# Forget-gate attention: the causal mask in the forget rows, a third bank for the scores, k's squares in halves, low weights by adding transfers

## The reference, cut to what matters

```python
q, k, v, z, f_logit = jnp.split(h @ w_in, ...)
q = rms_norm(q.reshape(b, s_len, 16, 128), q_norm_g)      # per head and token
k = rms_norm(k.reshape(b, s_len, 16, 128), k_norm_g)
c = jnp.cumsum(jax.nn.log_sigmoid(f_logit + f_bias), axis=1)
# per head, blocks of 128 queries:
logits = q_blk @ k.T * 128 ** -0.5 + c_blk[:, None] - c[None, :]
logits = jnp.where(k_pos <= q_pos, logits, -jnp.inf)
o = jax.nn.softmax(logits, axis=-1) @ v
out = (o * jax.nn.silu(z)) @ w_out
```

## Time and profile before

| | us |
|---|---|
| three runs, median (lowest, highest) | 2593.55 (2592.87, 2595.41) |
| profiled execution: span on the core | 2593.1 |
| TensorE busy (share of the span) | 2550.1 (98%) |
| VectorE, ScalarE, GpSimd busy | 1509.1, 1231.1, 1514.3 |

### The profile page before, as it was taken

One profiled execution on the slowest core, in us unless ns is written; L12 is line 12 of the kernel. 1 busy time (PEld: TensorE's weight loads), 2 busy tenths in 40 slices (PEclk: granted clock), 3 DMA queues, 4 the chain that ended last, 5 costly groups with the idle time before them and its releaser, 6 DMA issues.

```text
span 2593.1 us, 31711 instructions
## 1 busy us (share of the span) xinstructions
PE 2550.1 (98%) x12043; PEld 2055.1 (79%) x12043; DVE 1509.1 (58%) x2434; ACT 1231.1 (47%) x1944; POOL 1514.3 (58%) x935
## 2 busy tenths in 40 slices
PE   8999999999999999999999999999999999999998
PEld 6777787878778788888888887878876778788887
DVE  6999764165585714444450799976498744532202
ACT  5887645254564623222232588664335553422322
POOL 2999766444444366444455399966635547644653
PEclk9999999999999999999999999999999999999999
DMA  8776434434234133333333677543422242233221
GB/s 195 177 177 145 122 97 91 98 82 82 75 71 74 57 98 93 96 95 96 96 95 97 152 167 175 140 114 108 113 96 86 67 139 97 86 98 98 98 98 65
DMA packets 296440, 279.12 MB, mean 108 GB/s; under 512 B 17814, under 2 KB 258672, under 8 KB 296289
## 3 DMA queue, kind: packets, MB, share of 16 engines
q1 hardware_dynamic: 281472, 223.94, 31.0%
q0 software_dynamic: 14816, 53.16, 10.0%
HBM read 228.75 MB, written 5.84 MB: 90 GB/s over the span
## 4 chain that ended last, share of the span: by engine, by line
PE 82%; DVE 9%; ACT 4%; issue 2%; DMA 2%; POOL 1%; SPq 0%; DVEq 0%; POOLq 0%; ACTq 0%
PE ps L64 80%; DVE AR L81 4%; DVE AR L73 2%; PE ps L67 2%; DVE HL L81 1%; DMA WR<-in_a_w_in 1%; ACT L70 1%; ACT AR L70 1%; DMA WL<-WR 1%; ACT HT L70 1%; DVE X L73 1%; POOL AR L73 0%; DVE ps L81 0%; ACT WL L70 0%; ACT HH L70 0%
## 5 line engine op out<-in xcount | busy, mean ns | idle before, releaser
L73 POOL TENSOR_TENSOR WL<-WR,WH 128x1024 fp32r<-128x1024 f32 x324 | 818.8, 2547 | 762.6 <-ACT WH L70 762.6
L64 PE MATMUL ps<-HH,WH 128*128 128x512 f32 x3080 | 1226.7, 399 | 4.3 <-ACT HH L70 1.2
L64 PE MATMUL ps<-HL,WH 128*128 128x512 f32 x3080 | 1194.9, 391 | 1.3 <-DVE HL L81 1.3
L64 PE MATMUL ps<-HH,WL 128*128 128x512 f32 x3080 | 1096.1, 390 | 2.3 <-DMA WL<-WR 2.3
L64 PEld LDWEIGHTS ps<-HH,WH 128*128 128x128 f32 x3080 | 579.6, 188 | 146.6 <-issue 15.3
L64 PEld LDWEIGHTS ps<-HL,WH 128*128 128x128 f32 x3080 | 580.0, 188 | 127.0 <-issue 7.9
L64 PEld LDWEIGHTS ps<-HH,WL 128*128 128x128 f32 x3080 | 578.6, 188 | 123.8 <-DMA WL<-WR 2.7
L70 ACT ACTIVATE WH<-WR 128x1024 fp32r<-128x1024 f32 (+1 forms) x405 | 409.2, 1047 | 488.9 <-PE ps L64 443.0
L81 DVE SCALAR_TENSOR_TENSOR ps<-AR,CW,ps 128x512 f32<-128x512 f32 x654 | 454.6, 752 | 17.2 <-ACT ps L70 10.2
L73 POOL TENSOR_TENSOR AR<-AR 128x512 f32<-128x512 f32 x200 | 306.8, 1848 | 16.2 <-ACT AR L70 8.9
L70 ACT ACTIVATE AR<-ps 128x512 f32<-128x512 f32 (+3 forms) x265 | 131.9, 522 | 272.8 <-PE ps L64 176.5
(11 more groups left out here) (184 smaller groups left out, 2180.0 us busy)
## 6 DMA issues: line engine op xcount, KB each, us to landing
WR<-in_a_w_in SPq DMA_DIRECT2D x96, 512.0 KB, 5.2
WL<-WR POOLq DMA_DIRECT2D x81, 512.0 KB, 5.7
WR<-in_c_w_in SPq DMA_DIRECT2D x64, 512.0 KB, 5.4
WR<-in_a_w_out SPq DMA_DIRECT2D x16, 1024.0 KB, 4.9
WR<-in_b_w_in SPq DMA_DIRECT2D x16, 1024.0 KB, 8.4
WR<-in_b_w_in SPq DMA_DIRECT2D x32, 512.0 KB, 11.0
WR<-in_w_mlp_in SPq DMA_DIRECT2D x16, 1024.0 KB, 5.4
WR<-in_w_mlp_out SPq DMA_DIRECT2D x16, 1024.0 KB, 4.9
```

The costliest lines, as they stand in the source:

```text
L64: return Op(None if self.e is None else self.e.matmul(o, l, r, start=first, stop=last, skip_group_check=True))
L73: return Op(None if self.e is None else self.e.tensor_tensor(o, a, b, op))
```

## The change

The mask: `causal_gpsimd` sets -1e30 above the diagonal in CB itself, which is now one buffer of 1280 columns, a forget row of its own for each block (3, 2, 1, 0 in this order); the mask products, `caus` and `identr` go. `negc_rows` holds the rows in this layout, written by four stores. The select of `setup_gpsimd` for the mask goes, too. The scores: blocks 0, 1, 2, 3 use banks 4, 5, 2, 4 (head 15: 4, 5, 4, 5). k's squares: high and low halves as q's, by ScalarE, VectorE and GpSimd. Low weights: chunks of heads 1 to 15 are `summed`; GpSimd's and ScalarE's rounds take them half by half. QN and KN have one buffer, CB is fetched behind the last row maximum of the head before. MR, AR and DIAG are laid out anew.

```diff
         WL = sb("WL", 2 * 2048, F32R)
-        identr = sb("identr", P, F32R)
-        caus = sb("caus", P, F32R)
-        MR = sb("MR", 1280, F32R)
+        onesr = sb("onesr", P, F32R)
+        MR = sb("MR", 4 * T, F32R)
         ident = sb("ident", P)
...
-            return i == 0 and n == 1 or any(f < i < f + KE + (KE // 2 if n == 0 else 0) or i == f + KE + KE // 2 + 1 for f in FIRST_A)
+            return i == 0 and n == 1 or i in HEAD_CHUNK[1:] or any(f < i < f + KE + (KE // 2 if n == 0 else 0) or i == f + KE + KE // 2 + 1 for f in FIRST_A)
 
...
-            pool.memset(SM0, 0.0).then_inc(consts, "mask0")
-            pool.wait_ge(consts, "mask0")
+            pool.wait_ge(consts, "ident0")
             pool.select(ident[:, :], ALU.not_equal, 1.0, [[-1, P]], 1).then_inc(consts, "ident")
-            pool.select(SM0, ALU.is_ge, NEG, [[-1, P]], 1).then_inc(consts, "mask")
-            pool.wait_ge(consts, "mask")
-            pool.copy(identr[:, :], ident[:, :]).then_inc(consts, "identr")
-            pool.copy(caus[:, :], SM0).then_inc(consts, "caus")
             split_lo(pool, 0, (0,))
...
-        DIAG = [ar(A0 + 8 * T + i * P, P) for i in range(5)]
+        DIAG = [HT[:, i * P:(i + 1) * P] for i in range(5)]
...
-        b_cb = [sig("b_cb0"), sig("b_cb1")]
+        b_cb = sig("b_cb")
...
-        RAW, QN, KN, CB = ([ar(B1 + (2 * n + i) * T) for i in range(2)] for n in range(4))
-        NEGC = ar(B1 + 8 * T)
-        E8, BY2 = RB2, [RB, ar(B1 + 9 * T)]
-        LF, FB = ar(B1 + 10 * T, 64), ar(B1 + 10 * T + 64, 16)
-        BF, BAB, BEX, BMN = (ar(B1 + 10 * T + 80 + 64 * n, 64) for n in range(4))
-        TRI, FT = RAW[0], KN[0][0:16, :]
-        SQHI, SQLO, onesr = MR[:, 0:T], MR[:, T:2 * T], MR[:, 1024:1152]
-        negc_rows = nc.dram_tensor("negc_rows", (16, T), F32).ap()
-        V_CHUNK = [FIRST_B + 9 + 6 * g for g in range(4)]
-        HEAD_CHUNK = [FIRST_B + 9 + 6 * (h // 4) + 2 + h % 4 for h in range(16)]
+        RAW = [ar(B1 + i * T) for i in range(2)]
+        QN, KN = ar(B1 + 2 * T), ar(B1 + 3 * T)
+        CB, C_OFF = ar(B1 + 4 * T, 1280), [1152, 896, 512, 0]
+        NEGC = ar(B1 + 7 * T)
+        E8, BY2 = RB2, [RB, ar(B1 + 6 * T + 256)]
+        LF, FB = ar(B1 + 8 * T, 64), ar(B1 + 8 * T + 64, 16)
+        BF, BAB, BEX, BMN = (ar(B1 + 8 * T + 80 + 64 * n, 64) for n in range(4))
+        TRI, FT = RAW[0], KN[0:16, :]
+        SQHI, SQLO = ([MR[:, (2 * n + i) * T:(2 * n + i + 1) * T] for i in range(2)] for n in range(2))
+        negc_rows = nc.dram_tensor("negc_rows", (16, 1280), F32).ap()
 
         def values_tensor(pe, g):
             for part in range(2):
...
-                            pe.wait_ge(b_var, 4 * g - 2, 0)
+                            pe.wait_ge(b_ttr, 4 * g - 2, 2)
...
         def scores_tensor(pe, h):
-            s = h % 2
             pe.wait_ge(b_nrm, h, 0, 4)
             pe.wait_ge(b_nrm, h, 1, 4)
             for i in range(NB):
-                b, n = banks[4 + i % 2], (i + 1) * P
-                if i >= 2:
-                    pe.wait_ge(b_ttr, h, i - 2)
-                elif h:
-                    pe.wait_ge(b_ttr, h - 1, i + 2)
-                elif i:
-                    pe.wait_ge(b_e8)
+                if i == 0:
+                    pe.wait_ge(*((b_ttr, h - 1, 3) if h else (b_ft,)))
+                elif i == 1:
+                    pe.wait_ge(*((b_ttr, h - 1, 1) if h else (b_e8,)))
+                elif i == 2:
+                    pe.wait_ge(*((b_var, h, 0) if h < 15 else (b_ttr, h, 0)))
                 else:
-                    pe.wait_ge(b_ft)
-                pe.mm(b[:, 0:n], QN[s][:, i * P:(i + 1) * P], KN[s][:, 0:n], True, False)
-                pe.mm(b[:, i * P:n], identr[:, :], caus[:, :], False, True).then_inc(b_s, h, i)
+                    pe.wait_ge(b_ttr, h, 0 if h < 15 else 1)
+                pe.mm(logit_bank(h, i), QN[:, i * P:(i + 1) * P], KN[:, 0:(i + 1) * P], True, True).then_inc(b_s, h, i)
+
+        def logit_bank(h, i):
+            return banks[((4, 5, 2, 4) if h < 15 else (4, 5, 4, 5))[i]][:, 0:(i + 1) * P]
 
         def statistics_tensor(pe, h):
             if h == 0:
@@ -1501,10 +1497,12 @@
             else:
                 pe.wait_ge(b_var, h - 1, 0)
             pe.wait_ge(consts, "onesr")
+            if h:
+                pe.wait_ge(b_ttr, h - 1, 2)
             pe.wait_ge(b_sq, h, 0)
-            pe.wait_ge(b_sqlo, h, 1)
-            pe.mm(banks[2][:, :], onesr, SQHI, True, False)
-            pe.mm(banks[2][:, :], onesr, SQLO, False, True).then_inc(b_stat, h, 0)
+            pe.wait_ge(b_sqlo, h, 0, 1)
+            pe.mm(banks[2][:, :], onesr[:, :], SQHI[0], True, False)
+            pe.mm(banks[2][:, :], onesr[:, :], SQLO[0], False, True).then_inc(b_stat, h, 0)
             if h >= 2:
                 pe.wait_ge(b_ev, h - 2, 3)
             elif h == 1:
@@ -1512,7 +1510,9 @@
             else:
                 pe.wait_ge(rb_made, 1)
             pe.wait_ge(b_sq, h, 1)
-            pe.mm(banks[7][:, :], ones[:, :], SQS[1], True, True).then_inc(b_stat, h, 1)
+            pe.wait_ge(b_sqlo, h, 1, 1)
+            pe.mm(banks[7][:, :], onesr[:, :], SQHI[1], True, False)
+            pe.mm(banks[7][:, :], onesr[:, :], SQLO[1], False, True).then_inc(b_stat, h, 1)
...
         def normal_vector(dve, h):
-            s = h % 2
-            for half, (o, g) in enumerate(((QN[s], VQ[:, 0:1]), (KN[s], va["k_norm"]))):
+            for half, (o, g) in enumerate(((QN, VQ[:, 0:1]), (KN, va["k_norm"]))):
                 y, raw = BY2[half], RAW[half]
                 dve.wait_ge(b_y, h, 1, half)
-                if h >= 2:
-                    dve.wait_ge(b_s, h - 2, 3)
+                if h:
+                    dve.wait_ge(b_s, h - 1, 3)
                 dve.tt(o, y, y, ALU.mult).then_inc(b_nrm, h, half, 0)
                 dve.wait_ge(b_nrm, h, half, 0)
                 dve.stt(o, o, -0.5, VAR[half], ALU.mult, ALU.mult).then_inc(b_nrm, h, half, 1)
-                if half == 0:
-                    dve.wait_ge(b_sqlo, h, 0)
+                dve.wait_ge(b_sqlo, h, half, 0)
                 dve.stt(raw, raw, g, y, ALU.mult, ALU.mult).then_inc(b_nrm, h, half, 3)
                 dve.wait_ge(b_nrm, h, half, 3)
                 dve.stt(o, o, 1.5, raw, ALU.add, ALU.mult).then_inc(b_nrm, h, half, 4)
@@ -1620,13 +1618,13 @@
 
         def logits_vector(dve, h):
             small(4, "b_sum", h)
-            dve.wait_ge(b_cb[h % 2], h)
+            dve.wait_ge(b_mask, h, 1)
             for i in range(NB):
                 n = (i + 1) * P
                 dve.wait_ge(b_s, h, i)
                 if h:
                     dve.wait_ge(b_t, h - 1, i)
-                dve.ttr(BP[i], banks[4 + i % 2][:, 0:n], CB[h % 2][:, 0:n], -1.0, 3e38, ALU.add, ALU.min,
+                dve.ttr(BP[i], logit_bank(h, i), CB[:, C_OFF[i]:C_OFF[i] + n], -1.0, 3e38, ALU.add, ALU.min,
                         small(1, "b_max", h, i)).then_inc(b_ttr, h, i)
...
-                    split_hi(act, HEAD_CHUNK[h] + 1)
+                    split_hi(act, HEAD_CHUNK[h] + 1, (0,))
                     act.wait_ge(b_p, h, 0)
                     if h:
                         act.wait_ge(b_stat, h - 1, 0)
-                    act.act(SQHI, banks[0][:, :], ACT.Square).then_inc(b_sq, h, 0)
+                    act.act(SQHI[0], banks[0][:, :], ACT.Square).then_inc(b_sq, h, 0)
                 if h >= 2:
                     copy_turned_scalar(act, h - 2, 0)
                     copy_turned_scalar(act, h - 2, 1)
                 if h < 16:
+                    split_hi(act, HEAD_CHUNK[h] + 1, (1,))
                     act.wait_ge(b_p, h, 1)
                     if h:
                         act.wait_ge(b_stat, h - 1, 1)
-                    act.act(SQS[1], banks[1][:, :], ACT.Square).then_inc(b_sq, h, 1)
+                    act.act(SQHI[1], banks[1][:, :], ACT.Square).then_inc(b_sq, h, 1)
                 if h >= 2:
                     copy_turned_scalar(act, h - 2, 2)
                     copy_turned_scalar(act, h - 2, 3)
...
+        def forget_rows_gpsimd(pool, h):
+            pool.wait_ge(b_negc_out, NB - 1)
+            pool.dma(CB, bass.AP(negc_rows.tensor, h * 1280, [[0, P], [1, 1280]])).then_inc(b_cb, h, by=16)
+
+        def causal_gpsimd(pool, h):
+            pool.wait_ge(b_cb, h)
+            for n, (first, step) in enumerate(((384, 384), (1024, P))):
+                blocks = CB[:, first:first + 2 * step].rearrange("p (b c) -> p b c", c=step)[:, :, 0:P]
+                pool.select(blocks, ALU.is_ge, NEG, [[0, 2], [-1, P]], 1).then_inc(b_mask, h, n)
+
+        def square_low_gpsimd(pool, h, half):
+            pool.wait_ge(b_raw, h, half)
+            if h:
+                pool.wait_ge(b_stat, h - 1, half)
+                pool.wait_ge(b_sqlo, h - 1, half, 1)
+            pool.tt(SQS[half], RAW[half], RAW[half], ALU.mult).then_inc(b_sqlo, h, half, 0)
+            pool.wait_ge(b_sqlo, h, half, 0)
```

(41 more changed lines are left out.)

## The result

The change makes the kernel slower: 2614.54 us, median of 4 runs, against 2593.21 us before; the ratio is 1.008, 95% interval 1.0068 to 1.0092. The forecast was 2572.5 us. The profiled execution's span is 2616.3 us.

A forecast was written before the change was run, and what follows sets the result against it. TensorE, busy 2550.1 of 2593.1 us, was taken as the bound; ten plain intervals 18.5, three with values 4.1, start +0.5 and k's waits -1.8 sum to 21.3 us saved: 2572.5 us, range 2566 to 2584.

The forecast's parts named there:

- rival 4: Weight loads of the heads: no change, because shorter heads wait for loads that start later; 2593 us, chance 0.05.
- Rival 3: Low weights: adding transfers land late, at 11.0 us, so 13 heads wait 2.2 us each; 2601 us, chance 0.06.
- masks 0.52: Scores on TensorE: 64 mask products leave, 0.13 us a mask, saving 0.52 us a head.
- third bank 0.44: Block 2's scores, moved to bank 2, no longer wait for block 0's maximum: 0.44 us saved a head.
- k's sum 0.40: Sum of k's squares: two fp32r products replace one fp32 product of 512 columns, saving 0.40 us a head.
- hold-up 0.49: TensorE's wait for normalised k, made by GpSimd's subtractions holding up VectorE, goes: 0.49 us a head.
- The start: Head 0: 3.1 us of new waiting offset by a wait that goes; the next interval 18.7 us, +0.5 in all.
- k waits of 0.6 us: Second head after each values group: TensorE waits 0.6 us for k's low squares, three times, -1.8 us.
- Values intervals: Three head-to-head intervals with a values group have no wait before the scores: 1.36 us saved each, 4.1 in all.
- The tail: Last head: delayed early projection makes the last T 0.65 us later, the last scores give 0.65 back: 0.
- Rival 1: VectorE's chain: the hold-up only moves to GpSimd's selects and squares; heads 18.2 us apart, 2580 us, chance 0.12.
- Rival 2: GpSimd's queue bounds: every second head waits 2.6 us for k's low squares, some 10 us; 2582 us, chance 0.11.

The follow-up runs named there:

- the run with c_w_in's rows: Changed kernel with the heads' q and k weights fetched from c_w_in (rows 32,768 B apart, not 32,832 B; other values): 2582.4 us, ratio 0.995.
- the even pitch: Changed kernel with the q and k chunks fetched from the same b_w_in at a row pitch of 32,768 B instead of 32,832 B: 2582.8 us, 0.9955.
- the runs with repaired order: Changed kernel with whole chunks behind heads 3, 7, 11, 15 and `part_low` before the last forget rows: 2575.8 us with c_w_in's rows, 2608.7 with real rows.

## Why the prediction was wrong

- **The step that failed** is in the forecast's sentences on when the low weights are wanted and in rival 4: "Each next weight load starts some 5 us later than now; one takes 11.0 us and has about 19", "a load would have to take 19 us". 11.0 us is a median over halves, and over heads of which a half has faster loads. For heads 4 to 7 and 12 to 15 the k halves take 12.8 to 25.4 us in the trace of before, and in the changed kernel 13.4 to 26.0. I read the median and not the spread, which the same profile gives as 4.7/9.6/25.4.
- **The bound of the adding transfers**, 4.5 to 9.3 us, came from 81 transfers in other stages, beside loads with even pitch. Beside a slow load they took 12 to 24 us. Rival 3 had the mechanism (they land as the loads do), its price (11.0 us, from the same median) and a chance of 0.06. It named an argument against itself that did not bear: "none of the trace's 81 passed 9.3", when none of the 81 had such a load beside it: they belong to other mixers, whose loads of 512 KB have medians of 5.2 and 5.4 us. Rivals 3 and 4 also work together, which I hadn't joined: the next load waits until the adding transfer has left its slot, so one that is late makes the next load late.
- **Its size.** Interval by interval, in the profiled executions (spans 2616.3 and 2578.2 us; the medians are 32 us apart), the changed kernel loses 37.5 us to the run with c_w_in's rows. By the waits, TensorE stood 24.9 us for WL<-WR. The rest is laid to the clock: 0.95 in the stretch of 535 to 930 us against 0.98 in the run with c_w_in's rows and in that with the even pitch, 0.03 of 395 us, about 12 (a rough estimate, since idle time counts in it).
- **TensorE's terms** (masks 0.52, third bank 0.44, k's sum 0.40, hold-up 0.49) held together: 1.89 us measured against 1.85, in every undisturbed head. The four were not measured one by one. For the ten intervals: 19.0 against 18.5 us.
- **The start**: k's sum waited 3.5 us in head 0 (forecast 3.1). The next interval was 17.13 to 17.15, where I had 18.7: GpSimd was ready for it.
- **k waits of 0.6 us** in the second head behind a values group: none in the even-pitch run, the interval is 17.35. The forecast took 1.8 us off for nothing.
- **Values intervals**: 1.36 each forecast, 0.07 measured with c_w_in's rows (40.63 to 40.56). I had costed the half-by-half order at nothing; in the values rounds it puts the second half's subtraction behind q's squares. With the order repaired they gave 1.85, but took 1.6 from the head before.
- **The tail**: forecast 0, measured 7.4 us (22.0 against 14.6). I had seen `part_low` stand behind the last forget rows and priced it at 0.65 us for the next T, without asking what TensorE does meanwhile: nothing, and the clock falls.
- **Rival 1** (the hold-up only moves) holds for heads beside subtractions alone, at 2.79 us in the changed kernel's head 7 and at 18.99 in the runs with repaired order. **Rival 2** (GpSimd's queue) holds without the adding transfers: 30.1 us.

In sum, on loads that land in 4 to 9 us the time is 2582.4 us, and the forecast would have missed by 10 too. By intervals the tail was 7.4 us and the values rounds 3.9 short; the start, the k waits and the ten heads gave 3.9 back, so 13.9 us were gained of the 21.3. The other 32 us are the loads.

## What to carry to other kernels

A median time to landing says nothing of the transfers next to your change: read them one by one in the stretch, and least and most of each kind, before you let something wait for one. Before making a chain of load, adding transfer, product and next load, look whether loads of that stage are already slow and hidden; a hidden slow transfer becomes a wait as soon as another transfer runs beside it. Weights fetched in 512 B pieces whose row pitch is no multiple of 512 B deserve a look first of all, every column range by itself; where the layout can be chosen, try another pitch.

## What the runs showed of the hardware

- Loads of 512 KB in 512 B pieces at a row pitch of 32,832 or 32,704 B took up to 26.0 (changed kernel) and 25.3 us, against at most 9.1 at 32,768 B, whether the pieces start on a multiple of 512 B or 64 B behind one, and 9.5 at 32,256 B. While one crawled at 52 GB/s the DMA engines were busy about a third of the time. At 32,832 B the slow heads were 4 to 7 and 12 to 15, at 32,704 B 0 to 3 and 8 to 11.
- GpSimd's transfers issued beside such a load were late: one moved no packet for 12.6 us, and landed after 23.4 us instead of 4.5, 2 us before the load did. The Trainium skill, page "DMA: Bandwidth & Descriptors", section "Queues, rings and completion order", says that each DMA engine takes turns between queues packet by packet; by that rule the transfer should have had a share from the start, and from 620 to 630 us the trace shows none taken. What holds them back isn't shown.
- An idle stretch of TensorE of 3.2 us (612.8 to 616.0) was followed by some 6 us at a clock of 0.50, in which a product of 512 columns took 0.43 us from start to start instead of 0.23; that wait cost about 3 us more than its length.
